# Encoder layer with 32 routed experts: the experts' rows are weighted when copied out and added in HBM by the scatter, in place of two pages and two combining passes

## The reference

```
h = rmsnorm(x, norm_ffn_g)                       # x is the residual after the mixer
g_sel = argmax(h @ w_grp + b_grp)                # one of 4 groups of 8 experts
top_v, top_i = top_k(in_group_logits, 2)         # two experts inside that group
top_w = softmax(top_v) * group_probability
for e in range(32):
    hid = silu(h @ w_gate[e]) * (h @ w_up[e])
    y = y + combine[:, e:e+1] * (hid @ w_down[e])
out = rmsnorm(x + y, final_norm_g)
```

## Time and profile before

| | |
|---|---|
| median of three runs | 800.6 us |
| profiled execution | 800.86 us, its span (first to last instruction) 798.9 us |
| TensorE busy | 744.3 us (93%) |
| VectorE, ScalarE, GpSimd busy | 226.7, 146.1, 86.9 us |
| DMA | 234.71 MB, mean 294 GB/s; queue q1 (SP) 229.61 MB, q0 (GpSimd) 4.20 MB |
| granted TensorE clock, mean | 0.977 of full speed |

### The profile page before, as it was taken

How to read it: one execution, slowest core, us unless ns; L and a number is a source line. 1 busy time by engine, 2 the same in 40 slices (tenths; PEclk the granted TensorE clock), 3 DMA queues, 4 the chain that set the end, 5 groups by cost and what they waited for, 6 DMA issues and landing times.

```text
span 798.9 us, 13655 instructions
## 1 busy us (share of the span) xinstructions
PE 744.3 (93%) x6174; PEld 381.2 (48%) x6174; DVE 226.7 (28%) x447; ACT 146.1 (18%) x304; POOL 86.9 (11%) x78
## 2 busy tenths in 40 slices
PE   5999999999999997999999999999999899989960
PEld 4444454464455466455545455544445454434510
DVE  3017872005565266211111111111111111111116
ACT  5153330033354254000000000000000000000004
POOL 0632340000000022000000000000000000000002
PEclk9999999999999998999999999999999999999995
DMA  9321130410540737899999999999999999999955
GB/s 333 105 105 36 70 106 1 158 48 14 235 186 1 301 137 300 316 406 422 427 426 420 424 427 423 426 426 422 424 426 424 423 426 422 424 424 426 407 223 201
DMA packets 35243, 234.71 MB, mean 294 GB/s; under 512 B 5730, under 2 KB 7138, under 8 KB 18928
## 3 DMA queue, kind: packets, MB, share of 16 engines
q1 hardware_dynamic: 32624, 229.61, 70.5%
q0 software_dynamic: 2560, 4.20, 1.4%
HBM read 227.50 MB, written 10.49 MB: 298 GB/s over the span
## 4 chain that ended last, share of the span: by engine, by line
PE 73%; DMA 21%; DVE 3%; ACT 2%; issue 1%; SPq 0%; POOLq 0%; DVEq 0%
PE bank L470 21%; DMA arena<-in_w_up 19%; PE bank L769 18%; PE bank L792 9%; PE bank L752 7%; PE bank L638 4%; PE bank L682 3%; PE bank L599 1%; PE bank L671 1%; DMA arena<-y_tok 1%; PE bank L656 1%; PE bank L771 1%; PE bank L772 1%; PE bank L454 1%; PE bank L781 1%
## 5 line engine op out<-in xcount | busy, mean ns | idle before, releaser
L769 PE MATMUL bank<-arena 128*64 128x512 f32 x928 | 208.0, 601 | 13.7 <-DMA arena<-in_w_up 12.9
L470 PE MATMUL bank<-arena 128*128 128x512 f32 x384 | 167.0, 594 | 0.0
L769 PEld LDWEIGHTS bank<-arena 128*64 128x64 f32 x928 | 70.7, 138 | 146.9 <-issue 146.0
L1087 DVE TENSOR_TENSOR arena<-bank,arena 128x512 f32<-128x512 f32 (+1 forms) x96 | 47.8, 512 | 306.9 <-ACT arena L1046 215.1
L792 PE MATMUL bank<-arena 128*64 128x512 f32 x512 | 116.9, 598 | 0.5 <-ACT arena L1050 0.5
L470 PEld LDWEIGHTS bank<-arena 128*128 128x128 f32 x384 | 72.3, 190 | 89.8 <-issue 89.5
L752 PEld LDWEIGHTS bank<-arena 128*128 128x128 bf16 x3072 | 95.9, 98 | 24.4 <-issue 23.9
L752 PE MATMUL bank<-arena 128*128 128x64 bf16 x3072 | 100.2, 193 | 0.0
L1519 POOL DMA_INDIRECT y_tok<-arena x32 | 31.3, 978 | 435.1 <-DVE arena L1391 417.2
L1046 ACT ACTIVATE arena<-bank 128x256 f32<-128x256 f32 x32 | 12.3, 384 | 357.9 <-PE bank L769 325.3
L792 PEld LDWEIGHTS bank<-arena 128*64 128x64 f32 x512 | 33.9, 136 | 57.0 <-issue 54.8
(11 more groups left out here) (162 smaller groups left out, 480.5 us busy)
## 6 DMA issues: line engine op xcount, KB each, us to landing
arena<-in_w_gate SPq DMA_DIRECT2D x31, 2048.0 KB, 29.4
arena<-in_w_down SPq DMA_DIRECT2D x31, 2048.0 KB, 32.4
arena<-in_w_up SPq DMA_DIRECT2D x30, 2048.0 KB, 28.5
arena<-in_w_in SPq DMA_DIRECT2D x6, 2048.0 KB, 8.1
arena<-y_tok SPq DMA_DIRECT2D x8, 512.0 KB, 5.6
arena<-in_x SPq DMA_DIRECT2D x4, 512.0 KB, 5.7
arena<-in_w_out SPq DMA_DIRECT2D x2, 1024.0 KB, 8.1
arena<-in_w_out SPq DMA_DIRECT2D x1, 2048.0 KB, 21.9
```

What stands on the lines that cost most here:

```text
L470: m = pe.matmul(pbank[unit_bank(n)][:], lhs(k), rhs(k), start=(k == 0), stop=(k == KC - 1))
L769: mm = pe.matmul(both, xT[:, k], gate_and_up(e, k, cols), start=(k == 0), stop=(k == KC - 1))
L1087: return nc.vector.tensor_tensor(out_, a, b, op)
```

## The change

- `y_tok` goes; a tensor `x_acc` in HBM, one page of 512 tokens by two halves, takes its place. SP copies the four tiles of `x1` into it once they are complete, between gate of expert 3 and down of expert 2 on its queue.
- The scatter has an add as its operation: it adds each row of the buffer to the row of `x_acc`. GpSimd first waits for the four copies, and before each scatter for the one before it to have landed.
- A token's weight for an expert is carried to its slot by the product that makes the destinations. The weight is split into three bf16 parts, so that product has 160 columns in place of 64, and its factors are ready only after the weights are known. A reduction adds the three parts.
- `y_evict` multiplies by the slot's weight instead of copying.
- At the end SP waits for all scatters and reads the one page into `x1`'s place; ScalarE starts on a tile when it has landed. The passes L1462 and L1467 go, as do `later`, `sooner`, `page`, `comb_by`.

```diff
+            for t in range(TT):
+                sp.wait_ge(x1_done, 2 * (t + 1))
+                sp.dma_start(x_acc_d[t], x1[:, t]).then_inc(xacc_in, 16)
...
-            for k in range(2):
-                for s in range(RING):
-                    sp.wait_ge(y_stored[s], 16 * len(range(s, EXPERTS - 1 + k, RING)))
-                for t in range(TT):
-                    sp.dma_start(got[k][:, t], y_tok_d[k, t]).then_inc(later_in[t] if k else sooner_in, 16)
             sp.wait_ge(most_done, 1)
             general = sp.value_load(most[0:1, 0:1], min_val=0, max_val=T)
+            with sp.If(general < limit + 1):
+                for s in range(RING):
+                    sp.wait_ge(y_stored[s], 16 * len(range(s, EXPERTS, RING)))
+                for t in range(TT):
+                    sp.dma_start(x1[:, t], x_acc_d[t]).then_inc(sum_in[t], 16)
...
-                            mm = pe.matmul(pbank[7][64 * half:64 * half + 64, 0:2 * EXPERTS], by_slot[k][:, t],
+                            mm = pe.matmul(pbank[7][64 * half:64 * half + 64, 0:5 * EXPERTS], by_slot[k][:, t],
...
-                act.wait_ge(x2_done, t + 1)
+                act.wait_ge(sum_in[t], 16)
...
+                then(nc.vector.tensor_copy(w_part[0], comb))
+                then(tt(w_rest[0], comb, w_part[0], ALU.subtract))
+                then(nc.vector.tensor_copy(w_part[1], w_rest[0]))
+                then(tt(w_rest[1], w_rest[0], w_part[1], ALU.subtract))
+                then(nc.vector.tensor_copy(w_part[2], w_rest[1]))
+                for k in range(2):
+                    for i in range(3):
+                        m = tt(by_expert[k][:, :, 2 + i], hot[k], w_part[i][:, :, k:k + 1].broadcast_to((P, TT, EXPERTS)), ALU.mult)
+                m.then_inc(rows_split, 1)
...
-                nc.vector.tensor_copy(y_sb[e % RING], pbank[5 + e % RING][:]).then_inc(y_evicted, 1)
+                nc.vector.tensor_scalar(y_sb[e % RING], pbank[5 + e % RING][:], w_slot[:, e:e + 1], None, ALU.mult).then_inc(y_evicted, 1)
...
+                nc.vector.tensor_reduce(w_slot, pbank[7][:, 2 * EXPERTS:5 * EXPERTS].rearrange("p (i e) -> p e i", i=3), AX.X,
+                                        ALU.add).then_inc(rows_joined, 1)
...
-                for t in range(TT):
-                    nc.vector.scalar_tensor_tensor(got[0][:, t], got[0][:, t], comb_by[:, t, 0:1], x1[:, t], ALU.mult,
-                                                   ALU.add).then_inc(x2_half, 1)
...
-                    nc.vector.scalar_tensor_tensor(x2[:, t], got[1][:, t], comb_by[:, t, 1:2], got[0][:, t], ALU.mult,
-                                                   ALU.add).then_inc(x2_done, 1)
...
+            pool.wait_ge(xacc_in, 16 * TT)
             for e in range(EXPERTS):
                 pool.wait_ge(y_evicted, e + 1)
-                nc.gpsimd.indirect_dma_start(y_tok, bass.IndirectOffsetOnAxis(ap=tab_u[:, e:e + 1], axis=0), y_sb[e % RING], None,
-                                             bounds_check=last_row, oob_is_err=False).then_inc(y_stored[e % RING], 16)
+                if e >= 1:
+                    pool.wait_ge(y_stored[(e - 1) % RING], 16 * ((e - 1) // RING) + 16)
+                nc.gpsimd.indirect_dma_start(x_acc, bass.IndirectOffsetOnAxis(ap=tab_u[:, e:e + 1], axis=0), y_sb[e % RING], None,
+                                             bounds_check=last_row, oob_is_err=False, compute_op=ALU.add).then_inc(y_stored[e % RING], 16)
```

More of the change, by code:

```diff
@@ L88, in mixer_and_moe @@
         both_b = ctx.enter_context(nc.sbuf_tensor("both_b", [P, TT, EXPERTS], BF16))
-        y_tok = nc.dram_tensor("y_tok", [2 * T * 2, D // 2], F32).ap()
+        x_acc = nc.dram_tensor("x_acc", [T * 2, D // 2], F32).ap()
         def sem(name):
@@ L228, in down_unit @@
             return at(unit_kib[(3 * e + 2) % UNITS], FC, D)
-        got = [at(96, TT, D), at(112, TT, D)]
         res = at(16, TT, D)
@@ L240, in mixer_and_moe @@
         row_odd, half_col = tok_c[:, 2 * TT:2 * TT + 1], tok_c[:, 2 * TT + 1:]
-        later = extra[:, 80:84].unsqueeze(2)
-        sooner = extra[:, 84:88].unsqueeze(2)
-        page = extra[:, 88:96].rearrange("p (t k) -> p t k", k=2)
+        w_part = [extra[:, 80 + 4 * i:84 + 4 * i].bitcast(BF16).rearrange("p (t k) -> p t k", k=2) for i in range(3)]
+        w_rest = [extra[:, 92 + 8 * i:100 + 8 * i].rearrange("p (t k) -> p t k", k=2) for i in range(2)]
         by_slot = [at(207 + 0.5 * k, TT * SLOTS // 2).bitcast(BF16).rearrange("p (t s) -> p t s", t=TT) for k in range(2)]
-        by_expert = [at(208 + 0.5 * k, TT * EXPERTS).bitcast(BF16).rearrange("p (t a e) -> p t a e", t=TT, a=2) for k in range(2)]
-        comb_by = extra[:, 96:104].rearrange("p (t k) -> p t k", k=2)
-        part = extra[:, 104:112].rearrange("p (t k) -> p t k", k=2)
+        by_expert = [at(208 + 1.25 * k, TT * 5 * EXPERTS // 2).bitcast(BF16).rearrange("p (t a e) -> p t a e", t=TT, a=5)
+                     for k in range(2)]
+        w_slot = extra[:, 112:112 + EXPERTS]
         ident_b = at(206, P // 2).bitcast(BF16)
@@ L300, in mixer_and_moe @@
                                                             sem("d_done"), sem("y_evicted"))
-        sooner_in, later_in = sem("sooner_in"), [sem(f"later_in{t}") for t in range(TT)]
+        xacc_in, sum_in = sem("xacc_in"), [sem(f"sum_in{t}") for t in range(TT)]
         rows_split, rows_summed, rows_joined, dest_done = sem("rows_split"), sem("rows_summed"), sem("rows_joined"), sem("dest_done")
-        x2_half, x2_done = sem("x2_half"), sem("x2_done")
         res_done, out_stored = sem("res_done"), sem("out_stored")
@@ L319, in mixer_and_moe @@
         wd_d = w_down.rearrange("l e (h p c) d -> (l e) p h (c d)", h=2, c=2)
-        y_tok_d = y_tok.rearrange("(k t p h) d -> k t p (h d)", k=2, t=TT, h=2)
+        x_acc_d = x_acc.rearrange("(t p h) d -> t p (h d)", t=TT, h=2)
         def x1_by_chunk(t):
@@ L442, in _ @@
             sp.wait_ge(out_stored, 16 * TT)
-            sp.wait_ge(sooner_in, 16 * TT)
-            for t in range(TT):
-                sp.wait_ge(later_in[t], 16)
+            sp.wait_ge(xacc_in, 16 * TT)
         @block.tensor
@@ L819, in _ @@
                 if e == 2:
-                    pe.wait_ge(rows_joined, 2)
+                    pe.wait_ge(rows_joined, 3)
                 down(e)
@@ L1356, in slots_and_weights @@
                     nc.vector.tensor_scalar(by_expert[k][:, :, 1], hot[k], row_odd, None, ALU.mult)
[L1357 to L1363, removed]
+                    tt(by_expert[k][:, :, 0], hot[k], row_lo.broadcast_to((P, TT, EXPERTS)), ALU.mult)
                 dve.wait_ge(cexp_done, 1)
@@ L1403, in join_destinations @@
                 tt(tab_f, tab_f, pbank[7][:, EXPERTS:2 * EXPERTS], ALU.add).then_inc(rows_joined, 1)
-                dve.wait_ge(rows_joined, 2)
+                nc.vector.tensor_reduce(w_slot, pbank[7][:, 2 * EXPERTS:5 * EXPERTS].rearrange("p (i e) -> p e i", i=3), AX.X,
+                                        ALU.add).then_inc(rows_joined, 1)
+                dve.wait_ge(rows_joined, 3)
                 nc.vector.tensor_copy(tab_u, tab_f).then_inc(dest_done, 1)
@@ L1455, in _ @@
                 for t in range(TT):
-                    nc.vector.tensor_copy(x2[:, t, 0:1], x2[:, t, 0:1]).then_inc(x2_done, 1)
+                    nc.vector.tensor_copy(x2[:, t, 0:1], x2[:, t, 0:1]).then_inc(sum_in[t], 16)
                 for t in range(TT):
@@ L1459, in _ @@
             with dve.If(general < limit + 1):
-                dve.wait_ge(sooner_in, 16 * TT)
                 for t in range(TT):
-                    nc.vector.scalar_tensor_tensor(got[0][:, t], got[0][:, t], comb_by[:, t, 0:1], x1[:, t], ALU.mult,
-                                                   ALU.add).then_inc(x2_half, 1)
-                for t in range(TT):
-                    dve.wait_ge(x2_half, t + 1)
-                    dve.wait_ge(later_in[t], 16)
-                    nc.vector.scalar_tensor_tensor(x2[:, t], got[1][:, t], comb_by[:, t, 1:2], got[0][:, t], ALU.mult,
-                                                   ALU.add).then_inc(x2_done, 1)
-                    if t >= 1:
-                        final_norm(t - 1)
-                final_norm(TT - 1)
+                    final_norm(t)
         @block.gpsimd
@@ L1513, in _ @@
                                         h2_part[TT - 1][1][:, halves[h]], ALU.subtract).then_inc(parts_done, 1)
-            last_row = EXPERTS * SLOTS - 1
+            last_row = 2 * T - 1
             pool.wait_ge(dest_done, 1)
+            pool.wait_ge(xacc_in, 16 * TT)
             for e in range(EXPERTS):
                 pool.wait_ge(y_evicted, e + 1)
-                nc.gpsimd.indirect_dma_start(y_tok, bass.IndirectOffsetOnAxis(ap=tab_u[:, e:e + 1], axis=0), y_sb[e % RING], None,
-                                             bounds_check=last_row, oob_is_err=False).then_inc(y_stored[e % RING], 16)
+                if e >= 1:
```

(3 more changed lines are left out.)

## The result

The changed kernel takes 809.57 us in the median of four runs (808.49 to 811.02), the kernel before beside it 800.44 us. The ratio is 1.0107, with a 95% interval of 1.0088 to 1.0126: slower by 9 us, where 810 us was forecast.

A forecast was written before the change was run, and what follows sets the result against it. The prediction took the full DMA stream of the expert block as the bound. Its terms, -2.2 + 1.0 + 9.8 + 0.6 = +9.2 us, gave a forecast of 810 us, range 799 to 828 us.

The forecast's parts named there:

- What bounds the kernel: Expert block, 355 to 745 us: DMA engines full, so added DMA work comes out at the end one for one.
- The scatters in the block: Experts 1 to 28: each add reads the scatter's bytes once more, 28 x 0.35 = +9.8 us.
- q0's share near 2.7%: Sign that the forecast is right: the scatter queue's share of the DMA engines comes near 2.7%.
- The end: After the last copy-out: passes and second page go, -2.2 us; the last scatter's add costs +1.0 us.
- The front: Before the block: the product widened to 160 columns delays up of expert 4, so the block starts +0.6 us later.
- The copies and GpSimd's wait: Copies of x1 fit idle DMA time before the block; scatters land before the next is due: 0 us each.
- The copy-out: Multiplying instead of copying, same shape, 0.69 us before: 0 us, at most +0.1 once, on the last one.
- The free add: Rival, expert block: the add's read costs nothing in the full stream; 799.3 us, chance 0.24.
- Engines that stand still: Rival, expert block: DMA engines hold their pipe for each add, 48 us in place of 9.8; 848 us, chance 0.09.
- The chain of scatters: Rival, expert block: adding scatters take over 14.2 us to land and become the bound; 858 us, chance 0.05.
- TensorE's first wait: Sign that the forecast is right: in the block, TensorE first waits for an up load before 571 us.
- the waits sum: Sign that the forecast is right: TensorE's waits for up loads total near 22 us instead of 13.

The follow-up runs named there:

- e1_plain_write: The changed kernel with the scatter's add taken out, so it writes its rows over those of x_acc; ratio 0.9980, 798.8 us.
- e5_add_ends_only: The changed kernel with the add only in the scatters of experts 0, 29, 30 and 31; ratio 0.9988, 799.4 us.
- e7_reordered_end: The kernel before, with VectorE's first-page pass of tile 3 moved behind tile 0's second pass; ratio 0.9992.
- e2_twice_plain: The kernel before, with the plain scatter of experts 1 to 28 issued twice, the extra one to an unread tensor; ratio 1.0127, +10.2 us.
- e9_light_before: The kernel before, loading only half the down weights of experts 4 to 30; ratio 0.9781, 782.2 us.
- e11_half_size_rows: The kernel before, with the experts' rows in bf16 in the ring, both pages and the tiles read back; ratio 0.9929, -5.7 us.

## Why the prediction was right

*What bounds the kernel.* Right, and shown three ways: without the add the block is back at 407.8 us, with the rows written twice it is as long as with the add, and with room in the stream no price is left in the trace.

*The scatters in the block: +9.8 predicted, +9.0 measured*, 0.32 us each. The choice among 0, 0.35 and 1.7 us by the nearest row was right. The row shown for it was to be q0's share near 2.7%; it is 3.0%, (24.3 - 11.2) / 32 = 0.41 us more per scatter, above both the 0.35 and the 0.32. So the share overstates what the stream paid. Of 28 x 0.41 = 11.5 us, 0.7 us may have gone into the idle time of 335 to 345 us, where the share is now 1.00; where the rest went stays open. By the rule of the Trainium skill (Collectives: The Full Stack, The bandwidth ceiling), which it gives for the reduce step of a ReduceScatter, two source reads for an add at half a copy's rate, the engines' time for a scatter should double. The trace agrees, with 0.35 and 0.76 us.

*The end: -1.2 predicted, -1.3 measured* up to the first sum of squares. The sum fits by luck, as both of its terms were too large. With the plain scatter of e1_plain_write the first sum of squares comes 7.8 us after the last copy-out in place of 9.3: -1.5 where -2.2 was predicted. With the add it comes after 8.0 us, +0.2 where +1.0 was taken; in e5_add_ends_only after 8.4, +0.6. The last adding scatter lands after 4.0, 4.4 and 4.5 us in three executions, but plain ones land after 2.5 to 4.0 us in ten: the 2.7 us of the earlier trace rows was one value of a spread and no price of a plain scatter. The read's first tile arrives 3.2 us after its issue. That the gain was just VectorE's lateness behind the landing was argued and is not shown: e7_reordered_end removed that lateness and gained 0.1 us, since there tile 0 itself came at 781.8; what the end owes to the removed pass and what to a single page on the queue stays open. Missed: the final norm takes 15.3 us in place of 15.8. VectorE's multiplication of tile 2 takes 1.74 us in place of 2.33 and GpSimd's of tile 1 2.35 in place of 2.86; in e1_plain_write they take 1.75 and 2.35. That it is because VectorE has no second pass of tile 3 beside them any more is argued.

*The front: +0.6 predicted, +0.3 measured.* Timelines of the changed kernel, VectorE's last factors and TensorE's product:

```profile
325.00 1.30 DVE L1085 TENSOR_TENSOR arena<-arena 128x128 bf16<-128x128 f32 x6
```

```profile
329.00 0.74 PE L801 MATMUL bank<-arena 128*64 128x160 bf16 x16
```

The factors end at 326.3, 2.7 us before TensorE asks, so they are covered. The product takes 0.74 us; scaling the whole 0.44 by its columns gave 1.1, but a part of the 0.44 does not grow with them. From expert 0's first matmul to up of expert 4 it is 21.6 us in place of 21.3, in the changed kernel and in e1_plain_write alike.

*The copies and GpSimd's wait: 0 and 0*, both measured alone, to 0.2%.

*The copy-out* is 0.75 us in place of 0.69: +0.06 once, as bounded.

*The rivals.* The free add falls with e1_plain_write and e2_twice_plain. Engines that stand still would have given q0 over 5%. The chain of scatters never decided: 12.3 us at most against 14.2. By the Trainium skill (DMA: Bandwidth & Descriptors, Latency and other measured facts) an HBM access takes up to 2 us under high load, which made 10 us of 8.0. The trace is a little above it: the median landing grew by 2.8 us, to 10.8.

*The signs.* TensorE's first wait came before 571 us (519.30), and the waits sum to 22.5 us where 22 was named. That sum was a weak sign: with one slow-clock round more it would have been 20.8, as e2_twice_plain's 20.9.

*How exact it was.* Forecast and median difference are 9.2 and 9.1 us, but the terms measured in the profiles, +9.0, -1.3, -0.5, +0.3 and +0.1, make 7.6: the block was 0.8 us shorter than forecast, the front 0.3, and the final norm's 0.5 was missed. The interval, 7.0 to 10.1 us, holds both, and no run tells them apart; a front that starts late more often would fill the gap and is not shown.

## What to carry to other kernels

Ask of every byte that a change moves whether it falls into a stretch where the DMA stream is full and has no gap: there it was paid almost in full (0.33 us for a plain scatter's share of 0.35, 0.32 us for an add's of 0.41), an add in the DMA as a second passage of its rows, and passes saved on idle engines behind that stretch paid little back. In such a stretch look for rows that can be narrower before looking for clever ways to move them. Measure a stage's excess by the distance between like instructions, not by the sum of its waits: a round at the lower clock takes its time out of the waits. Do not take a single landing time for a price; look at how it spreads over executions first.

## What was not expected of the hardware

An adding scatter is not only longer on the DMA engines. Its issue on GpSimd takes 1.54 us in place of 0.97, and it makes 144 packets in place of 80 for the same rows; its landing under load grows by 2.8 us, while with idle engines behind the last expert it lies at 4.0 to 4.5 us beside 2.5 to 4.0 for a plain one. A plain issue is not always 0.97 us either: the last one takes 1.98 us in e9_light_before and e11_half_size_rows, where VectorE's passes run at the same time. A table loaded ahead on ScalarE does not last past an operation of another table: a second load stood before the square and a third before the root. TensorE's start of expert 0 moved by 2.7 us between executions of like front ends (317.09 and 319.78 us), more than a quarter of the effect studied: such a shift has to be taken off before a stage is charged with it.
